# Second pass of a chunked RWKV-7 layer: the inverse kept in the other partition half than its transpose, a level's two products on four array tiles with a bank each

## The reference

```
def step(state, inp):
    r_t, w_t, k_t, v_t, a_t, b_t = inp
    sa = jnp.einsum('bhvk,bhk->bhv', state, a_t)
    state = (state * w_t[:, :, None, :] + sa[..., None] * b_t[:, :, None, :]
             + v_t[..., None] * k_t[:, :, None, :])
    y = jnp.einsum('bhvk,bhk->bhv', state, r_t)
    return state, y
```

## Time and profile before

| what | value |
|---|---|
| median of 3 runs | 2746.04 us |
| span of the profiled execution, first to last instruction | 2741.6 us |
| PE busy | 2435.3 us (89%) |
| PEld (weight loads) busy | 1526.5 us (56%) |
| DVE busy | 1125.0 us (41%) |
| ACT busy | 756.1 us (28%) |
| POOL busy | 391.0 us (14%) |
| `L1095`, PE, 64x64 products, 8704 records | 299.9 us busy, 222 ns mean |

### The profile page before, as it was taken

The page is one execution under the profiler, slowest core; times in us unless marked ns, Lnnn a source line. Parts: engine busy times, 40 slices in busy tenths (PEclk is TensorE's granted clock), DMA queues, the critical chain, the costliest instruction groups (busy, mean ns, idle before and its releaser), DMA issues. The chain is left out here.

```text
span 2741.6 us, 67298 instructions
## 1 busy us (share of the span) xinstructions
PE 2435.3 (89%) x27710; PEld 1526.5 (56%) x27711; DVE 1125.0 (41%) x2596; ACT 756.1 (28%) x1815; POOL 391.0 (14%) x481
## 2 busy tenths in 40 slices
PE   3999999999997799999999997389999999998970
PEld 1878778788786657777777674223333333232220
DVE  0355555556556345656565654411111111111118
ACT  0244454453443112222323231012222212121212
POOL 0111111111111211212121120001010101010100
PEclk6999999999998899999999998589999999999985
DMA  8012121121123543222222221565535386999959
GB/s 329 9 47 93 47 81 60 47 93 47 47 86 126 232 186 112 78 107 81 100 84 100 90 87 39 245 269 229 222 138 229 138 350 237 395 362 401 379 224 369
DMA packets 54676, 451.78 MB, mean 165 GB/s; under 512 B 7933, under 2 KB 8993, under 8 KB 32577
## 3 DMA queue, kind: packets, MB, share of 16 engines
q1 hardware_dynamic: 36504, 390.71, 36.2%
q0 software_dynamic: 10656, 38.80, 3.7%
q10 hardware_dynamic: 7304, 19.19, 1.9%
HBM read 367.41 MB, written 87.56 MB: 166 GB/s over the span
## 5 line engine op out<-in xcount | busy, mean ns | idle before, releaser
L1755 PE MATMUL ps<-arena 128*32 128x512 f32 x4608 | 514.6, 604 | 25.5 <-DMA arena<-wex 20.5
L1755 PEld LDWEIGHTS ps<-arena 128*32 128x32 f32 x4608 | 150.5, 112 | 383.0 <-issue 367.5
L452 PE MATMUL ps<-arena 128*128 128x128 f32 x3072 | 354.9, 276 | 8.6 <-ACT arena L593 8.6
L452 PEld LDWEIGHTS ps<-arena 128*128 128x128 f32 x3072 | 349.3, 193 | 21.4 <-ACT arena L593 21.4
L1095 PE MATMUL ps<-arena 64*64 64x64 f32 x8704 | 299.9, 222 | 29.7 <-ACT arena L1312 9.1
L1095 PEld LDWEIGHTS ps<-arena 64*64 64x64 f32 x8704 | 279.8, 137 | 59.2 <-issue 57.6
L1769 PE MATMUL ps<-arena 128*32 128x512 f32 x2304 | 267.3, 605 | 8.3 <-DMA arena<-wex 5.6
L1254 PE MATMUL ps<-arena 128*128 128x512 f32 x496 | 229.2, 605 | 0.7 <-ACT arena L1332 0.7
L1975 DVE TENSOR_TENSOR arena<-arena,ps 128x256 f32<-128x256 f32 x72 | 29.9, 415 | 462.0 <-ACT arena L1813 462.0
L463 PE MATMUL ps<-arena 128*128 128x512 f32 (+1 forms) x512 | 213.5, 555 | 0.0
L1813 ACT ACT_TABLE_LOAD x36 | 46.2, 1283 | 586.6 <-PE ps L1755 586.6
(11 more groups left out here) (329 smaller groups left out, 3001.6 us busy)
## 6 DMA issues: line engine op xcount, KB each, us to landing
arena<-wex SPq DMA_DIRECT2D x105, 2048.0 KB
mid<-arena SPq DMA_DIRECT2D x16, 2568.0 KB, 8.5
arena<-mid SPq DMA_DIRECT2D x16, 2568.0 KB, 9.7
arena<-ada SPq DMA_DIRECT2D x12, 2048.0 KB, 9.3
arena<-y SPq DMA_DIRECT2D x16, 1024.0 KB, 7.4
arena<-x SPq DMA_DIRECT2D x31, 512.0 KB, 5.6
arena<-w_in SPq DMA_DIRECT2D x8, 1232.0 KB, 25.2
arena<-x ACTq DMA_DIRECT2D x17, 512.0 KB, 10.7
```

The lines of the kernel that those rows point to most:

```text
L452: mm = pe.matmul(bank[name][0:m, at:at + P], V["w_in"][:, kk, w0:w0 + m], V["hT"][:, kk, :], start=(kk == 0), stop=(kk == KD - 1))
L1755: mm = pe.matmul(bank[("HA", "HB")[g]][rows[j], :], xT[:, kk, rows[j]], slot[j][:, at:at + 2 * FH], start=(kk == 0), stop=(kk == KD - 1))
```

## The change

Three things change, all of them in the second pass.

1. *Placement.* X of chunk q now lies in the other partition half, `chunk[1 - q]`, while XT stays in `chunk[q]`. The triangular matrix in `MT` and the blocks `ET[l]` lie in `chunk[1 - q]` too, as `M` writes them there. For that, each of `M`'s products of key `BT` (f = 0), 128 columns wide before, is two of 64 columns, one into each half. Level 0 on DVE puts XT's first value into `Z` instead of `XX`.
2. *Tiles.* The product for X reads chunk q and writes half 1 - q; the product for XT reads chunk q and writes half q. `Xl` issues them in turn, head by head, and so uses four array tiles where it used two. `Zl` reads half 1 - q and writes half q, two tiles as before. `x2` now makes both X and XT by products with the identity, 32 products instead of 16.
3. *Banks.* X goes to X0 and X1, XT to YE and YO, 256 columns each. ACT copies each bank by itself: four copies of 256 columns a level instead of two of 512, four instead of two for `x2`; two at level 5, as before. `Yv` waits for the banks YE and YO until the last XT is read, and `x2` until `mean` has read them.

```diff
@@ -929,9 +929,9 @@
 _LV = range(1, len(LEVELS))
 USES2 = {"Z0": ("M", *(f"z{l}" for l in _LV), "G", "U0", "U1"),
          "Z1": ("M", *(f"z{l}" for l in _LV), "I", "U0", "U1"),
-         "X0": ("M", "t0", *(f"x{l}" for l in _LV), "WT"),
-         "X1": ("M", "t0", *(f"x{l}" for l in _LV), "WT", "D0", "D1"),
-         "YE": ("y",), "YO": ("y",),
+         "X0": ("M", "t0", *(f"x{l}" for l in _LV[:-1]), "WT"),
+         "X1": ("M", "t0", *(f"x{l}" for l in _LV[:-1]), "WT", "D0", "D1"),
+         "YE": ("t0", *(f"x{l}" for l in _LV), "y"), "YO": ("t0", *(f"x{l}" for l in _LV), "y"),
          "O0": ("yT", "o", "hT", "rl"), "O1": ("yT", "o", "hT")}
 BANK2 = {b: i for i, b in enumerate(("O0", "O1", "Z0", "Z1", "X0", "X1", "YE", "YO"))}
...
     MT, XX, Z, ET = W["MT"], W["XX"], W["Z"], W["ET"]
-    X, XT = (lambda rows, h: XX[rows, h // 4, 0, CHUNK * (h % 4):CHUNK * (h % 4) + CHUNK],
-             lambda rows, h: XX[rows, h // 4, 1, CHUNK * (h % 4):CHUNK * (h % 4) + CHUNK])
+
+    X, XT = (lambda q, h: XX[chunk[1 - q], h // 4, 0, CHUNK * (h % 4):CHUNK * (h % 4) + CHUNK],
+             lambda q, h: XX[chunk[q], h // 4, 1, CHUNK * (h % 4):CHUNK * (h % 4) + CHUNK])
     St = split(V["S"], CC)
     half = lambda h: (64 * (h % 2), h // 2)
...
     by_head = lambda ap: ap.rearrange("p (c e n) -> p c e n", c=CC, e=2)
     M_BANKS = (("Z0", "Z1"), ("X0", "X1"))
+    LEVEL_BANKS = (("X0", "YE"), ("X1", "YO"))
     MODS = len(ADA_PIECES) - MOD1
...
@@ -1079,29 +1081,48 @@
                                 for e, name in enumerate(M_BANKS[g]):
                                     hd = slice(64 * e, 64 * e + 64)
                                     at = P * c + CHUNK * q
-                                    mm = pe.matmul(split(bank[name][chunk[q], 256 * i + 128 * f:256 * i + 128 * f + 128], 2),
+                                    to = 256 * i + 128 * f
+                                    if f == 0:
+                                        pe.matmul(bank[name][chunk[1 - q], to:to + CHUNK], pk[key][hd, at:at + CHUNK],
+                                                  pk["AR"][hd, c, 0, chunk[q]], start=True, stop=True)
+                                        pe.matmul(bank[name][chunk[q], to + CHUNK:to + 2 * CHUNK], pk[key][hd, at:at + CHUNK],
+                                                  pk["AR"][hd, c, 1, chunk[q]], start=True, stop=True)
+                                        continue
+                                    mm = pe.matmul(split(bank[name][chunk[q], to:to + 2 * CHUNK], 2),
                                                    pk[key][hd, at:at + CHUNK], pk["AR"][hd, c, :, chunk[q]],
                                                    start=True, stop=True)
                                     if i == f == q == 1:
                                         B.full(mm, name)
                 return go
 
-            def blocks(name, lhs, rhs, heads, at=0, first=True, last=True):
-
-                if first:
-                    pe.sem_inc(S["pe_passed"], 1)
+            def blocks(name, lhs, rhs, heads):
+
+                pe.sem_inc(S["pe_passed"], 1)
                 for i, h in enumerate(heads):
-                    for rows in chunk:
-                        mm = pe.matmul(bank[name][rows, at + CHUNK * i:at + CHUNK * i + CHUNK], lhs(rows, h), rhs(rows, h),
+                    for q in range(2):
+                        mm = pe.matmul(bank[name][chunk[q], CHUNK * i:CHUNK * i + CHUNK], lhs(q, h), rhs(q, h),
                                        start=True, stop=True)
-                if last:
-                    B.full(mm, name)
+                B.full(mm, name)
+
+            def level_out(name, half, h):
+                return bank[name][chunk[half], CHUNK * (h % 4):CHUNK * (h % 4) + CHUNK]
 
             def x2(n, b):
                 for g in range(2):
                     S.wait(pe, "xt2", 2 * n + g + 1)
-                    B.wait_free(pe, f"X{g}", "t0", n)
-                    blocks(f"X{g}", XT, lambda rows, h: k("ident64")[rows, :], range(4 * g, 4 * g + 4))
+                    for name in LEVEL_BANKS[g]:
+                        B.wait_free(pe, name, "t0", n)
+                    pe.sem_inc(S["pe_passed"], 1)
+                    for h in range(4 * g, 4 * g + 4):
+                        for r in range(2):
+                            mm = pe.matmul(level_out(LEVEL_BANKS[g][0], r, h), Z[chunk[r], h, :], k("ident64")[chunk[r], :],
+                                           start=True, stop=True)
+                            if h % 4 == 3 and r == 1:
+                                B.full(mm, LEVEL_BANKS[g][0])
+                        for r in range(2):
+                            mm = pe.matmul(level_out(LEVEL_BANKS[g][1], 1 - r, h), k("ident64")[chunk[r], :], Z[chunk[r], h, :],
+                                           start=True, stop=True)
+                    B.full(mm, LEVEL_BANKS[g][1])
 
             def Zl(l):
                 def go(n, b):
@@ -1112,29 +1133,39 @@
                             S.wait(pe, "et1", 2 * n + g + 1)
                         B.wait_read(pe, f"X{g}", f"x{l - 1}" if l > 1 else "t0", n)
                         B.wait_free(pe, f"Z{g}", f"z{l}", n)
-                        blocks(f"Z{g}", lambda rows, h: ET[l][rows, h, :], X, range(4 * g, 4 * g + 4))
+                        blocks(f"Z{g}", lambda q, h: ET[l][chunk[1 - q], h, :], X, range(4 * g, 4 * g + 4))
                 return go
 
             def Xl(l):
                 def go(n, b):
                     for g in range(2):
-                        heads = range(4 * g, 4 * g + 4)
+                        own, turned = LEVEL_BANKS[g]
                         B.wait_read(pe, f"Z{g}", f"z{l}", n)
-                        B.wait_free(pe, f"X{g}", f"x{l}", n)
+                        B.wait_read(pe, turned, f"x{l - 1}" if l > 1 else "t0", n)
                         if l < last:
-                            blocks(f"X{g}", XT, lambda rows, h: Z[rows, h, :], heads, last=False)
-                        blocks(f"X{g}", lambda rows, h: Z[rows, h, :], XT, heads, at=256, first=(l == last))
+                            B.wait_free(pe, own, f"x{l}", n)
+                        B.wait_free(pe, turned, f"x{l}", n)
+                        pe.sem_inc(S["pe_passed"], 1)
+                        for h in range(4 * g, 4 * g + 4):
+                            if l < last:
+                                for q in range(2):
+                                    mm = pe.matmul(level_out(own, 1 - q, h), XT(q, h), Z[chunk[q], h, :], start=True, stop=True)
+                                if h % 4 == 3:
+                                    B.full(mm, own)
+                            for q in range(2):
+                                mm = pe.matmul(level_out(turned, q, h), Z[chunk[q], h, :], XT(q, h), start=True, stop=True)
+                        B.full(mm, turned)
                 return go
 
...
             def Wt(n, b):
                 pk = W["pk"][b]
                 for g in range(2):
-                    B.wait_read(pe, f"X{g}", f"x{last}", n)
+                    B.wait_read(pe, LEVEL_BANKS[g][1], f"x{last}", n)
                 for q in range(2):
...
@@ -1300,16 +1331,18 @@
         def _(act):
             def x2(n, b):
                 for g in range(2):
-                    B.wait_full(act, f"X{g}", "t0", n)
-                    B.free(act.activation(XX[:, g, 0, :], bank[f"X{g}"][:, 0:256], ACT.Copy), f"X{g}")
+                    for o, name in enumerate(LEVEL_BANKS[g]):
+                        B.wait_full(act, name, "t0", n)
+                        B.free(act.activation(XX[:, g, o, :], bank[name][:, 0:256], ACT.Copy), name)
 
             def Xl(l):
-                o = 1 if l == last else 0
-
                 def go(n, b):
                     for g in range(2):
-                        B.wait_full(act, f"X{g}", f"x{l}", n)
-                        B.free(act.activation(XX[:, g, o:, :], split(bank[f"X{g}"][:, 256 * o:], 2 - o), ACT.Copy), f"X{g}")
+                        for o, name in enumerate(LEVEL_BANKS[g]):
+                            if l == last and o == 0:
+                                continue
+                            B.wait_full(act, name, f"x{l}", n)
+                            B.free(act.activation(XX[:, g, o, :], bank[name][:, 0:256], ACT.Copy), name)
                 return go
 
...
                                                  k("mmask").unsqueeze(1).to_broadcast([P, 2, 4 * CHUNK]), ALU.mult), name)
                     dve.drain()
                     hd = slice(4 * g, 4 * g + 4)
-                    xt = split(XX[:, g, 1, :], 4)
+                    xt = Z[:, hd, :]
                     dve.tensor_tensor(xt, MT[:, hd, 0:CHUNK], level[:, 0:1, :].to_broadcast([P, 4, CHUNK]), ALU.mult)
                     dve.drain()
                     dve.tensor_tensor(xt, xt, k("ident64").unsqueeze(1).to_broadcast([P, 4, CHUNK]),
```

6 lines of the change are left out of this document (3 added, 3 removed).

## The result

The changed kernel takes 2763.47 us (median of 7 runs, 2753.73 to 2765.61) against 2746.04 (2742.47 to 2753.38) of the kernel before in the same comparison: ratio 1.0059, 95% interval 1.0045 to 1.0072. It is slower by 17 us; forecast was 17 us faster, and the range ended at 2743. The profiled span is 2761.6 us, 20.0 more.

What follows compares the result with a forecast made beforehand. PE is nearly saturated, but DVE arrives with it, so a faster PE finds DVE late. 14 bodies at 1.10 us give 15.4, plus 2 for the first tiles: 2746.0 - 17.4 = 2728.6 us; range 2714 to 2743.

Steps and rivals of the forecast that it cites:

- the rate: Level products on four array tiles: 14.5 ns a record taken, with 29.7 as the far bound.
- Rival 4: x2, X1 to X4 and M: four tiles not fed faster than two, about +1.5 us a body, 2770 us; chance 0.09.
- The prediction's 1.98 us: A level's 32 products at the skill's 62 ns per MATMUL, gaining nothing; the prediction cited the trace against it.
- +0.15: M's products of key BT split in two: between nothing and +1.0 us a body, taken as +0.15.
- the walk: Timing followed from x2's first record to route: gain 0.98 us at h2T, 1.25 us at route.
- first effect, a loss of 0.45 us: ACT's nrm moves behind x2's fourth copy, then DVE's var and res1; level-2 evacuation at 5.56 instead of 5.11 us.
- DVE takes over: The forecast case, DVE late for a faster PE: gain 0.6 to 1.7 us a body, 2720 to 2737 us; chance 0.70.
- after it nothing changes its length: Behind route, Z5, X5, Wg, Yv, Wt, Wi and scans keep their length; the 1.25 us gain stays, less 0.15 for M.
- rival 3: Gain eaten by M at two-tile speed (+1.0 us) or supply stalls: 0.25 us a body left, 2740.5 us; chance 0.15.
- The two first tiles: Bodies of tiles 0 and 1, with ada pieces beside their levels: 2 us gain on the first, 0 on the second.

Runs made afterwards that it cites:

- 1: Changed kernel with a group's eight products of X issued before its eight of XT, two array tiles at a time: 2755.95 us, ratio 1.0036.
- 12: Changed kernel with o12 to o15 among x2, Z1, X1, turned x2 products merged, route behind Z5, two tiles at a time: 2739.01 us; four-tile twin 2754.45.
- 7: Changed kernel issuing two tiles at a time, with long output products o12 to o15 moved behind x2: 2738.44 us, ratio 0.9973.
- 5: Changed kernel with long output products o12 to o15 moved from ahead of x2 to among x2, Z1 and X1: 2739.54 us, ratio 0.998.
- 13 to 16: Changed kernel with 16, 32, 48 or 64 increments once before the loop, moving instruction-block borders: 2761.27, 2775.32, 2769.23 and 2773.07 us.
- the merged `x2`: Changed kernel, x2's turned products one of 256 columns per half and group: alone 2764.15 us; with o12 to o15 moved behind x2, 2755.31 us.

## Why the prediction was wrong

**Right: the rate.** `x2`'s 64 records in the long body run from 1491.09 to 1492.03 (timeline; the first and the last pair):

```profile
1491.09 0.27 PE L1118 MATMUL ps<-arena 64*64 64x64 f32 x2
...
1492.03 0.22 PE L1123 MATMUL ps<-arena 64*64 64x64 f32 x2
```

0.94 / 63 = 14.9 ns a record at the upper clock, with 14.5 forecast. Rival 4, four tiles at the pace of two, is out, although the time (2763) fell next to its 2770. The 62 ns per MATMUL of the Trainium skill ("TensorE: Matmul & The Clock Gate", "Back-to-back issue gap"), which the page gives for hardware decode off, are not seen here: the 64 MATMUL records of 32 products in a row took 14.9 ns each, two to a product. The prediction's 1.98 us counted one MATMUL to a product; with the two that the trace shows the page's figure would give an estimated 3.97. No run here shows which decode was on. M's 96 records took about 1.94 us from first start to last, the 64 before 1.87: +0.1, where +0.15 was taken.

**Right, with a wrong size: the walk.** In the body of 1445.35, which stops little before `route` (timeline, DVE, then PE):

```profile
1450.43 0.75 DVE L1445 TENSOR_TENSOR arena<-ps,arena 128x256 f32<-128x256 f32 x2
```

```profile
1455.44 1.09 PE L1297 MATMUL ps<-arena 128*128 128x128 f32 x8 [0.64 <-DVE arena L1533]
...
1457.01 1.15 PE L1103 MATMUL ps<-arena 64*64 64x64 f32 x31 [0.29 <-issue]
1459.95 1.98 PE L1304 MATMUL ps<-arena 128*128 128x36 f32 x16 [0.39 <-DVE arena L1521]
```

The level-2 evacuation stands 5.08 us after `x2`'s start; forecast 5.56, and 5.11 before. The "first effect, a loss of 0.45 us" did not come: ACT's unwaited copies follow each other every 0.28 us (x4 in 1.21), not every 0.46 as I had taken over from copies that waited for PE. `h2T` stands at 10.09 (forecast 10.20, before 11.18) and `route` at 14.60 (forecast 14.27, before 15.52), held by DVE's `h2` as said; the 0.29 us stop between them is in that. Over all bodies the stop-free period fell by 1.24 us, with the slower clock still in it, and by the estimate from the 65 bodies the change brought 1.4; forecast 1.10. That they agree so well is in part luck, since the 1.24 holds a loss that the walk did not have. DVE takes over, as the forecast said, and some 16 us in 13 periods were there to be had.

**Wrong: the step "after it nothing changes its length", and with it the sum of the forecast, which had no term for instruction supply.** In its place the runs showed 42.4 us of stops at instruction borders in 13 bodies instead of 9.6, and behind them 41.0 us at the lower clock where the prediction had read full clock and kept it. The sentence in rival 3, that stalls such as the 1.20 us of the earlier trace rows might come more often, named the mechanism, gave it no price, and bounded it by the other costs of that rival at 2740.5. The price of the stops was to be had from the trace of before. Level part: 602 matmul records, so 1204 instructions or 4.7 blocks in 22.07 us, one block in 4.7 us. Eight stops of 0.6 to 1.5 us stand at borders there, 3.8 to 5.8 us (median 5.0) behind the border before, so it was at the edge already. The change puts 64 more instructions into `x2` and shortens each X group (the 64 more of `M` come ahead of the level part). A stretch of four-tile products alone uses up 256 instructions in 128 x 14.5 ns = 1.9 us. After the change the level part is 1268 instructions, 5.0 blocks. At 4.9 us a block that is 24.3 us if nothing is in store when it begins, 19.4 if one block is; the walk had it at about 21. So the supply alone allowed anything from no loss to 3 us a body, and 2.5 us of stops a body more were measured. A term of that size in the sum would have made the forecast a toss-up instead of 0.8 for faster. The clock had no such warning in the trace of before, where it never fell in these periods.

The Trainium skill, "Runtime: NRT & Kernel Launch", "Instruction fetch mechanics", says that instructions come in 16 KiB blocks and that crossing a border is mostly hidden. The blocks are as it says (q8's packets); hidden they are in the kernel before (9.6 us in 13 bodies), not in this one (42.4).

**The two first tiles.** +2 us of gain were put on them. The first full body's `x2` came 1.7 us earlier.

**The cause, as far as it was shown.** That PE stops at instruction-block borders, and that the lower clock came behind those stops, is read from the profiles; no run has stops of that size at the full clock, so their shares, 20 and 15 us of loss, are an estimate. That pace within a stretch matters is shown by 1 and 12 against their four-tile twins (the same instructions, 7.5 and 15 us faster), and by the stops alone in 7 against 5 (21.5 instead of 33.5 us, times that can't be told apart); that thinning the stretch helps, by 5 and 7; that places matter, by 13 to 16. Open is why a packet starts 1.1 to 4.5 us after a border rather than at once, and why the merged `x2` took away what the order of 5 had gained.
